# Weight matrices of a decoder layer handed over in blocks of one load

## The reference

```
h = rmsnorm(x);  proj = h @ w_in          # w_in: 2048 x 8208
gdn  = gated DeltaNet(q, k, v, beta, g)   # 8 heads of 128, chunks of 64, short causal conv
hgrn = HGRN2(q, k, v, log f)              # 8 heads of 128, chunks of 64
x = x + concat(gdn, hgrn) @ w_out         # 2048 x 2048
x = x + relu(rmsnorm(x) @ w_up)^2 @ w_down   # 2048 x 8192, 8192 x 2048
y = rmsnorm(x)                            # and the new states
```

## Time and profile before

| | |
|---|---|
| median of 3 runs | 2934.77 us (2921.52 to 2938.18) |
| profiled execution | 2932.76 us, of it span 2930.5 us |
| mean granted TensorE clock | 0.991 |
| PEld, DVE, ACT, POOL busy | 2791.7, 2055.3, 1138.1, 312.9 us |
| bytes moved by DMA, packets | 396.66 MB, 516484 |
| packets under 2 KB | 484196 |
| q1 (SP's loads) | 462272 packets, 267.95 MB, 45.1% of 16 engines |
| q8 and q14 (instructions) | 179 and 61 packets, 2.93 and 0.50 MB |
| w_in, w_out, w_up, w_down block, issue to landing (median) | 8.8, 4.0, 4.7, 6.0 us |
| store to mix_scratch from tmp, load from rows_scratch (median) | 5.9, 7.8 us |

### The profile page before, as it was taken

One profiled execution on the slowest core, in us unless ns is written; L12 is line 12 of the kernel. 1 busy time (PEld: TensorE's weight loads), 2 busy tenths in 40 slices (PEclk: granted clock), 3 DMA queues, 4 the chain that ended last, 5 costly groups with the idle time before them and its releaser, 6 DMA issues.

```text
span 2930.5 us, 53943 instructions
## 1 busy us (share of the span) xinstructions
PE 2869.1 (98%) x22712; PEld 2791.7 (95%) x22712; DVE 2055.3 (70%) x2929; ACT 1138.1 (39%) x1432; POOL 312.9 (11%) x447
## 2 busy tenths in 40 slices
PE   9999999989999999999999999999999999999998
PEld 8999988879999999999999999999998999999998
DVE  6666655637575757575587777777778878887885
ACT  4333332323333323334344444444444444444454
POOL 4111111011111011102100000000000000000111
PEclk9999999989999999999999999999999999999999
DMA  8454569845463557445344454455477666666665
GB/s 211 72 89 76 89 72 73 73 61 98 63 102 68 100 59 96 90 137 161 103 137 136 151 156 145 136 158 156 135 237 224 190 192 202 187 193 196 197 190 203
DMA packets 516484, 396.66 MB, mean 135 GB/s; under 512 B 18930, under 2 KB 484196, under 8 KB 516244
## 3 DMA queue, kind: packets, MB, share of 16 engines
q1 hardware_dynamic: 462272, 267.95, 45.1%
q0 software_dynamic: 22672, 88.35, 8.3%
q10 hardware_dynamic: 31300, 36.93, 4.0%
HBM read 308.80 MB, written 84.37 MB: 134 GB/s over the span
## 4 chain that ended last, share of the span: by engine, by line
PE 81%; DVE 9%; issue 3%; ACT 3%; DMA 2%; ACTq 0%; SPq 0%; DVEq 0%; POOL 0%; POOLq 0%
PE main L1383 40%; PE main L1012 26%; PE mx L1383 7%; DVE w_lo L1983 1%; PE mx L1084 1%; PE mx L1265 1%; PE mx L1171 1%; PE mx L1160 1%; DMA tmp<-rows_scratch 1%; DMA mix_scratch<-tmp 1%; DVE tmp L2104 1%; PE mx L1143 1%; PE mx L1100 0%; PE mx L1273 0%; ACT tmp L1573 0%
## 5 line engine op out<-in xcount | busy, mean ns | idle before, releaser
L1012 PE MATMUL main<-h_hi,w_hi 128*128 128x296 f32 (+1 forms) x2592 | 608.5, 316 | 4.8 <-DVE h_lo L1995 2.2
L1383 PE MATMUL main<-forms_a,w_hi 128*128 128x288 f32 x3024 | 606.2, 296 | 4.7 <-DVE w_lo L2596 4.5
L1383 PE MATMUL main<-forms_b,w_hi 128*128 128x288 f32 x3024 | 603.9, 295 | 0.5 <-DVE w_lo L2596 0.5
L1012 PE MATMUL main<-h_hi,w_lo 128*128 128x296 f32 (+1 forms) x2592 | 564.9, 299 | 4.6 <-issue 4.6
L1012 PE MATMUL main<-h_lo,w_hi 128*128 128x296 f32 (+1 forms) x2592 | 565.5, 300 | 0.0
L1383 PEld LDWEIGHTS main<-forms_a,w_hi 128*128 128x128 f32 x3024 | 487.2, 189 | 6.8 <-DVE w_lo L2596 6.8
L1383 PEld LDWEIGHTS main<-forms_b,w_hi 128*128 128x128 f32 x3024 | 484.5, 188 | 0.7 <-DVE w_lo L2596 0.7
L1383 PE MATMUL main<-forms_a,w_lo 128*128 128x288 f32 x1512 | 448.2, 296 | 0.0
L1012 PEld LDWEIGHTS main<-h_hi,w_hi 128*128 128x128 f32 x2592 | 415.0, 190 | 33.2 <-issue 17.9
L1383 PE MATMUL main<-forms_b,w_lo 128*128 128x288 f32 x1512 | 445.1, 294 | 0.0
L1012 PEld LDWEIGHTS main<-h_hi,w_lo 128*128 128x128 f32 x2592 | 422.8, 190 | 0.0
(11 more groups left out here) (409 smaller groups left out, 3422.5 us busy)
## 6 DMA issues: line engine op xcount, KB each, us to landing
w_raw<-in_w_in SPq DMA_DIRECT2D x128, 512.0 KB, 8.8
w_raw<-in_w_up SPq DMA_DIRECT2D x128, 512.0 KB, 4.7
w_raw<-in_w_down SPq DMA_DIRECT2D x100, 512.0 KB, 6.0
u_forms<-ub POOLq DMA_DIRECT2D x32, 1152.0 KB, 6.1
z<-x_scratch SPq DMA_DIRECT2D x32, 576.0 KB, 6.3
x_scratch<-z POOLq DMA_DIRECT2D x31, 576.0 KB, 5.8
stage<-u_forms ACTq DMA_DIRECT2D x30, 576.0 KB, 4.0
w_raw<-in_w_out SPq DMA_DIRECT2D x32, 512.0 KB, 4.0
```

The costliest lines, as they stand in the source:

```text
L1012: ins = mm(out[:, half, :], w[:, ring, k, :], x[:, kx, half * width:half * width + width], start=first and n == 0, stop=last_ and n == 2)
L1383: ins = mm(out, w[:, k, :], x[:, kx, :], start=i in (0, 1, 3) and k == 0 and n == 0, stop=k == KP - 1 and n == 2, skip_group_check=True)
```

## The change

Each weight matrix is rearranged on the host before the launch, so that the block of one load lies in HBM as [128 partitions, 8, 128] in one piece: 128 pieces of 4 KB in the place of 1024 of 512 B. The gate columns become an array of their own, `w_gates`, with 8 x 16 numbers (512 B) in one piece per partition. The arrays are: w_in [head, unit, partition, 8, 128], w_out [tile, half, partition, 8, 128], w_up [tile, parity, partition, 8, 128], w_down [tile, parity, partition, 32, 128], of which a load takes 8 neighbours of the 32 (4 KB), or two parts where the window wraps. The loads are the same in number, size, destination and order.

```diff
-        w_in = io["w_in"][0].rearrange("(k p) n -> p k n", p=P)
-        w_out = io["w_out"][0].rearrange("(k p) n -> p k n", p=P)
-        w_up = io["w_up"][0].rearrange("(k p) n -> p k n", p=P)
-        w_down = io["w_down"][0].rearrange("(k p) n -> p k n", p=P)
+        w_gates, w_in, w_out, w_up, w_down = (io[n] for n in ("w_gates", "w_in", "w_out", "w_up", "w_down"))
...
-                sp.dma_start(w_raw[:, j, :, 0:2 * HEADS], w_in[:, UK * j:UK * j + UK, 4 * GK:4 * GK + 2 * HEADS]).then_inc(s_w[j], 16)
+                sp.dma_start(w_raw[:, j, :, 0:2 * HEADS], w_gates[j]).then_inc(s_w[j], 16)
...
-                    j = unit_order(h, i)
-                    col = (0 if j < 8 else HG0) + (j % 8) // 2 * GK
-                    k0 = UK * (j % 2)
-                    src = (w_in[:, k0:k0 + UK, col + h * P:col + h * P + P] if isinstance(h, int)
-                           else w_in[:, k0:k0 + UK, bass.ds(h * P + col, P)])
-                    load(src, h * 16 + (2 + i), (2 + i) % RAW)
+                    load(w_in[h, unit_order(h, i)], h * 16 + (2 + i), (2 + i) % RAW)
...
-                load(w_out[:, k0:k0 + UK, m * P:m * P + P], OUT_U0 + v, (OUT_U0 + v) % RAW)
+                load(w_out[m, k0 // UK], OUT_U0 + v, (OUT_U0 + v) % RAW)
...
-                    src = w_up[:, j % 2:KT:2, (2 * p + j // 2) * P:(2 * p + j // 2) * P + P]
+                    src = w_up[2 * p + j // 2, j % 2]
...
-                        src = w_down[:, 2 * q + j % 2:2 * (q + n_ - 1) + j % 2 + 1:2, m * P:m * P + P]
+                        src = w_down[m, j % 2, :, q:q + n_, :]
...
+def blocks(w, order):
+
+    return w.reshape(-1, P, w.shape[1] // P, P).transpose(2, 0, 1, 3).reshape((w.shape[1] // P,) + order + (P, P))
+
+
+def laid_out(inputs):
+
+    a = {name: inputs[name] for name in _INS}
+    w = a["w_in"][0]
+    tiles = w[:, 0:4 * GK], w[:, HG0:]
+    a["w_gates"] = w[:, 4 * GK:HG0].reshape(2, UK, P, 2 * HEADS).transpose(0, 2, 1, 3)
+    a["w_in"] = stacked([t.reshape(2, UK, P, 4, HEADS, P).transpose(4, 3, 0, 2, 1, 5) for t in tiles])
+    a["w_out"] = blocks(a["w_out"][0], (2, UK)).transpose(0, 1, 3, 2, 4)
+    for name in ("w_up", "w_down"):
+        a[name] = blocks(a[name][0], (a[name].shape[1] // P // 2, 2)).transpose(0, 2, 3, 1, 4)
+    return a
```

More of the change, by code:

```diff
@@ L2771, with stacked @@
         "final_norm_w"]
+def blocks(w, order):
[10 more added lines that the diff above has]
+    return a
+def stacked(parts):
+    import numpy as _np
+    return _np.concatenate(parts, axis=1).reshape(HEADS, 16, P, UK, P)
 _OUTS = [("y_prompt", (1, NP_, D)), ("y_sample", (SB, ST, D)), ("conv_prompt", (1, 1, PRE, 3 * GK)),
@@ L2784 @@
     arrays, io = {}, {}
-    for name in _INS:
-        a = _np.ascontiguousarray(inputs[name])
+    for name, a in laid_out({name: _np.asarray(inputs[name]) for name in _INS}).items():
+        a = _np.ascontiguousarray(a)
         arrays[f"in_{name}"] = a
```

## The result

| | before | after |
|---|---|---|
| median | 2932.28 us (4 runs) | 2887.99 us (4 runs, 2887.37 to 2890.2) |
| ratio, 95% interval | | 0.9854 (0.9824 to 0.9885) |
| span of the profiled execution | 2930.5 us | 2888.5 us |
| mean granted clock | 0.991 | 0.996 |
| DMA packets | 516484 | 147333 |

A forecast was written before the change was run, and what follows sets the result against it. TensorE, busy 2869.1 of 2930.5 us, was taken as the bound, with stalls and lower clock in two heads blamed on slow w_in packets: 2932.8 - 44.3 - 1.0 - 2.0 = 2885.5, say 2886 us, range 2868 to 2908.

The forecast's parts named there:

- The heads: Head stretches: faster w_in packets remove the excess of two long heads, 22.2 + 18.9, and 3.2 us of the last: 44.3 us.
- both ways of pricing: A w_in load in blocks: 1.4 us of each engine at q0's rate, taken, or 1.9 us at w_up's 29 ns per 512 B.
- The 4 KB piece: w_in loads: 178 ns per 4096 B at the rate of q0's transfers, bringing the weights' DMA share in a head to 15%.
- The turn: From w_up to w_down, where ScalarE waits for a block: gain between 0 and 4.9 us, taken as 2.
- The gate columns: Start, loads ahead of x: 64 B pieces become 512 B, gain between 0 and 1.07 us, taken as 1.0.
- The MLP: w_up and w_down steps: loads hidden behind the products, steps stay 22.3 us, gain 0 outside the turn.
- the first: Heads: slowness isn't w_in's layout, or packets were already at line rate; 2930 to 2933 us, chance 8%.
- the second: Two long heads: fetch stalls and clock loss go but another long wait stays, keeping some 20 of 41 us; about 2906, 7%.
- the third: Heads, turn and start: all heads' idle time (11 us), the whole turn and the start go too; 2871 us, 4%.
- the fourth: MLP: one contiguous piece concentrates 16 engines on one memory stretch, each of 256 blocks 3.4 us late; 3756 us, 3%.
- The two rules: DMA page: line rate from 512 B would leave w_in no gain; large power-of-two pitches slow, a rule used for no number.

The follow-up runs named there:

- b_not_win: After with w_in and the gate columns as in before, the other three matrices in blocks: 2921.78 us, ratio to before 0.9982.
- g_heads_moved: After with w_in in rows of 32832 B, gate columns in the middle, head h's columns where head (h+4) mod 8 had them: 2911.77 us, 0.9958.
- c_block_512: After with each w_in block lying tile by tile in one 512 KB stretch, read in 512 B pieces: 2888.02 us, ratio to before 0.986.
- d_pitch_32768: After with w_in in rows again, without the gate columns, rows 32768 B apart, 512 B pieces: 2888.29 us, ratio to before 0.986.
- f_pitch_32832: After with w_in in rows of 32832 B, the 16 numbers at the row's end, not in the middle: 2920.38 us, ratio to before 0.9982.
- a_win_only: After with the blocks of w_out, w_up and w_down taken back, only w_in and gate columns in blocks: 2892.26 us, ratio to before 0.9878.
- j_gates_packed: After with the gate columns packed on the receiving side too, 512 B in one piece per partition: 2887.77 us, ratio to before 0.9865.
- o_gates_apart_only: Before with the gate columns in their own array, so w_in's rows are 32768 B apart, and no blocks: 2891.21 us, ratio to before 0.9877.
- e_pitch_33024: After with w_in in rows of 33024 B, pieces starting at multiples of 512 B or 256 B behind them: 2885.87 us, ratio to before 0.9858.

## Why the prediction was right, step by step

**The heads: 44.3 us forecast, 42.7 measured.** The two long heads gave 22.2 and 18.3 us where 22.2 and 18.9 were forecast (168.55 and 165.21 to 146.34 and 146.91), and the last distance gave the 3.2 us that were forecast for it (149.48 to 146.32). One distance grew by 1.0 us, from 146.94 to 147.93. After has no idle time of TensorE above 1.5 us in its heads; what grew here is 5 us at a lower clock, with the engine busy throughout:

```profile
856.00:861.00 5.00, 5.00 (x30) 4.92 (x28) 4.07 (x8) 0.60 (x1) 0.41 (x1) 0.66 0.00 0
```

Ahead of it the engine is idle for 0.56 us behind VectorE (before 854.09), as it is in the other heads; what brought the clock down in this one is open. The sum had no term for the stretch behind the last run of 24, which gave 2.4 us more: TensorE is busy for 167.85 us there in the place of 169.64, at a clock of 1.00 in the place of 0.99, and idle for 0.6 us less.

**What I said of the cause was half of it.** That w_in's layout and the address decide, and not a busy memory, stands (b_not_win, g_heads_moved). That fewer and larger pieces cure it, which the sum used to price the new load, does not: it is the pitch (c_block_512, d_pitch_32768). The time came out all the same because both ways of pricing, 1.4 us and w_up's 1.9 us a load, are far below what a head can stand; for this part of the reason the forecast was lucky. The 4 KB piece was priced at 178 ns and measured at 195 ns or somewhat more; q1's share of the head is 19.2% and not 15%.

**Luck in the sum.** Against the profiled execution 47.3 us were forecast and 42.0 came, 1.6 less in the heads, 4.9 less at the start and 2.8 less at the end, against 2.4, 1.5 and 0.2 more in the stretches between. The medians differ by 44.3 us, but those of before alone lie between 2923.75 and 2932.28 us from group to group, so that they do not tell the sum to better than some 8 us.

**How slow packets stopped TensorE.** The weights were never late: no wait of ScalarE for a w_in block is in the profile of before. The others on the DMA engines were late. The two long heads as windows, first of before, then of after:

```profile
362.45:531.00 168.55, 152.62 (x1264) 143.62 (x1263) 95.62 (x179) 49.28 (x70) 22.45 (x30) 0.95 0.76 71
531.00:696.21 165.21, 151.48 (x1264) 142.50 (x1263) 95.82 (x179) 49.29 (x70) 21.62 (x30) 0.94 0.66 74
```
```profile
366.38:512.72 146.34, 145.26 (x1264) 137.35 (x1263) 95.47 (x179) 49.33 (x70) 21.50 (x30) 1.00 0.27 83
512.72:659.63 146.91, 145.53 (x1263) 137.37 (x1263) 96.52 (x179) 49.32 (x70) 21.73 (x30) 1.00 0.28 82
```

Of the 40.5 us between the pairs 27.2 are idle time and 13.3 are the same matmuls at a lower clock; the prediction had read 26 and 19 us from shorter windows, with a part counted in both. Three stalls with no releaser make up 20.1 us of the idle time, the pieces "issue" of 5.41, 4.57 and 10.11 us at 433.26, 510.32 and 594.25. The long pieces of the earlier trace rows cost far less than they are long, since TensorE ran beside them: behind the store of 16.93 us it waited 3.98 us (at 497.26, for `tmp` of VectorE), behind the gate rows of 18.15 us 0.87 us (at 571.33). I had counted four pieces "issue" in which TensorE stood still; the fourth, 3.77 us at 472.19, is none of them. TensorE's matmuls run through it without a gap, and the chain is on GpSimd there, which waits for VectorE before it issues the store:

```profile
476.00 0.18 POOL L192 TENSOR_TENSOR pool_spare<-pool_spare 1x1 f32<-1x1 f32 x1 [3.33 <-DVE tmp L2227]
```

The longest stall, in TensorE's instructions, and three stretches of the DMA of before, 594.3:602, 602:603.1 and 603.1:604.4, the last of which ends as TensorE goes on:

```profile
604.36 1.28 PE L1160 MATMUL mx<-tmp 128*64 128x32 f32 x18 [10.11 <-issue]
```

```profile
q1 hardware_dynamic: 1304, 0.66, 81.2%
```
```profile
q1 hardware_dynamic: 187, 0.09, 37.6%
q8 instruction: 1, 0.02, 5.2%
```
```profile
q1 hardware_dynamic: 155, 0.08, 23.0%
```

Through 7.7 us no instruction packet moves while SP's queue holds the engines; then one does, and TensorE resumes 1.3 us after the end of that stretch. The pieces of 5.4 us at 433.26 and 4.6 us at 510.32 end the same way, with one q8 packet in 436.2:437.3 and in 512.4:513.6 and none in the 2.9 and 2.0 us before. The other kernels with the slow pitch show the same. Between 190 and 1300 us before, b_not_win, f_pitch_32832 and g_heads_moved have eleven stalls of over 1.5 us without a releaser; each ends 2.1 to 2.6 us after the start of a q8 packet, the only one from 3 us before the stall to its end. After and d_pitch_32768 have no such stall. These are agreements in time, not an experiment on the fetch. The clock follows the stalls, in before's windows 594.2:604.4 and 604.4:620:

```profile
594.20:604.40 10.20, 0.09 (x3) 0.04 (x2) 0.23 (x1) 0.00 (x0) 0.00 (x0) 0.61 0.70 83
604.40:620.00 15.60, 15.60 (x142) 14.03 (x143) 4.00 (x8) 2.08 (x5) 3.10 (x2) 0.60 0.01 3
```

**The turn: 2 us forecast out of 0 to 4.9; 3.5 measured**, and 4 by a_win_only against after. In before ScalarE waited for a form (10.98 us, at 2200.46) and then for the block of w_down. In after it waits for the form alone, and the block that follows is there:

```profile
2162.43 0.93 ACT L1876 ACTIVATE forms_a<-forms_a 128x864 fp32r<-128x864 f32 x1 [14.26 <-DMA forms_a<-u_forms]
2163.26 1.04 ACT L1811 ACTIVATE w_hi<-w_raw 128x1024 fp32r<-128x1024 f32 x1
```

TensorE's idle time between the two steps of the table fell from 4.88 to 2.14 us. I had gone by the engine time of the block alone (0.5 us each) and not by the queue, where the blocks stand between the loads of the forms. That each shorter one lets the next form start sooner is my account; no run separates it.

**The gate columns: 1 us forecast, none found.** The step was wrong where it said that pieces of 64 B become 512 B, since the receiving side was still in pieces; and packing them there too (j_gates_packed) gained nothing either. In the profiled execution of after the start is even 3.9 us later. It is a matter of when x lands: TensorE waited 2.09 us before its first turn of x and then ran at clock 0.66 in 10:15.

```profile
10.13 0.34 PE L1033 MATMUL mx<-ident,x_tok 80*128 80x80 f32 x1 [2.09 <-POOL masks L772]
```

In before the first turn of x began at 7.79 us, without that wait, and the clock in 10:15 was 1.00. Kernels with the same start as after have the run that is at 220.06 there at 216.57 (o_gates_apart_only) to 219.27 us (e_pitch_33024), and those with the start of before have it at 216.13 and 218.45 (b_not_win), so most of this is the spread between executions. GpSimd is named as the releaser, but its L772 writes `masks`, which this instruction doesn't read; in the program it waits for x's load.

**The MLP: no change forecast**, and its steps take 22.3 us as before. ScalarE's 28 waits for w_down's blocks in before, 80.5 us in all, are gone in after, and outside the turn this bought nothing.

**The rivals.** None of the four came: not "no change" (the first), not 2906 us (the second), not 2871 us (the third), and not the slower MLP (the fourth).

**The two rules.** The Trainium skill, page "DMA: Bandwidth & Descriptors", section Specifications, has transfers at line rate from 512 B on. c_block_512 and d_pitch_32768 agree in so far as pieces of 4 KB were only some 4% cheaper per byte, once the pitch is right; whether 512 B in 28 ns is the line rate no run here shows. The same page's warning of large powers of two (section "Latency and other measured facts") is of the row pitch from partition to partition, in copies with pitches of 512 KiB and more. I had set it against the distance between tiles inside a partition, which is 8 MiB in w_up and 4 MiB in d_pitch_32768; a packet costs 29 and 28 ns there. The pitch from partition to partition is 32 KB in both, so no run here tests that rule.

## What to carry to other kernels

When a kernel on one engine shows stretches of different length for the same instructions, compare one recurring piece of the chain and the time per DMA packet in those stretches; slow packets of a prefetch that is itself never late can still cost the engine time, here through small transfers beside it and, by the agreements in time above, through its instructions. If the packets' cost changes with the column that is read, try another row pitch first: dropping 16 columns gave 2891.21 us here (0.9877), and a new layout of four matrices 2887.99 us (0.9854). A rearranged source makes larger pieces only where the destination is in one piece too.

## What was not expected of the hardware

- A row pitch of 32832 B made 512 B reads cost 141 ns in one head of eight and 50 to 89 ns in others; 32768, 33024, 33280 and 33344 B gave 28 to 30 ns. The slow head was the same in the profiles of before (141 ns), b_not_win (140 ns) and f_pitch_32832 (146 ns), and moved with the columns in g_heads_moved.
- 512 B and 4 KB pieces of HBM reads on this queue cost nearly the same per byte here (20.0% against 19.2% of the engines for the same bytes).
- The time of before spreads over 0.7% (2917.73 to 2937.43 us in 13 runs on one chip), that of after over 0.1% in 4 runs. In three profiles with the slow pitch the last stall took 10.11, 5.39 and 9.28 us (before, b_not_win, f_pitch_32832, one execution each), while the packets' cost stayed within 140 to 146 ns.
